# A hybrid attention and mixture-of-experts block on one core: y leaves PSUM in four blocks of 32 rows, the token sum runs in two row tiles of 64, and the expert kept outside the ring is number 23

## The reference, cut to what matters

```python
def _moe(x, router_w, router_bias, w_gate, w_up, w_down, sh_gate, sh_up, sh_down):
    ...
    def body(acc, blk):
        tok, w, e = blk
        xb = xf[tok]
        h = jax.nn.silu(xb @ w_gate[e]) * (xb @ w_up[e])
        return acc.at[tok].add((h @ w_down[e]) * w[:, None]), None
    ...
    shared = (jax.nn.silu(xf @ sh_gate) * (xf @ sh_up)) @ sh_down
    return (routed + shared).reshape(B, S, D)

for layer in range(2):
    h = mixer(x)
    x = _layer_norm(ALPHA * x + h, ...)
    f = _moe(x, ...)
    x = _layer_norm(ALPHA * x + f, ...)
```

## Time and profile before

| | us |
|---|---|
| median of three runs | 1326.66 (1326.54 to 1328.49) |
| the profiled execution, its own time | 1328.11 |
| its span in the trace | 1326.30 |
| TensorE busy | 1206.6 (91%) |
| DVE, ACT busy | 365.1 (28%), 257.3 (19%) |
| gate/up matmuls (L755), busy | 460.5 + 14.1 |
| down matmuls (L780), busy | 233.8 + 7.3 |
| DMA | 444.39 MB, 335 GB/s over the span |

### The profile page before, as it was taken

How to read it: one execution, slowest core, us unless ns; L and a number is a source line. 1 busy time by engine, 2 the same in 40 slices (tenths; PEclk the granted TensorE clock), 3 DMA queues, 4 the chain that set the end, 5 groups by cost and what they waited for, 6 DMA issues and landing times.

```text
span 1326.3 us, 15983 instructions
## 1 busy us (share of the span) xinstructions
PE 1206.6 (91%) x6187; PEld 556.8 (42%) x6187; DVE 365.1 (28%) x741; ACT 257.3 (19%) x544; POOL 16.0 (1%) x22
## 2 busy tenths in 40 slices
PE   8989999999999998999878799999999998999984
PEld 4556453433434343434344654443434344343431
DVE  0575451212112121212142436321212121111214
ACT  1343221111111111112102632121111111111110
POOL 0000000000000000000010001000000000000000
PEclk9996999999999999999979899999999999999997
DMA  9345439999999999999863406599999999999991
GB/s 338 77 171 242 166 129 380 420 419 420 420 419 420 421 420 422 420 421 420 334 248 127 190 2 261 218 420 418 420 421 419 419 420 421 420 421 420 421 379 64
DMA packets 67728, 444.39 MB, mean 335 GB/s; under 512 B 7648, under 2 KB 12128, under 8 KB 16352
## 3 DMA queue, kind: packets, MB, share of 16 engines
q1 hardware_dynamic: 67680, 443.71, 82.1%
HBM read 442.63 MB, written 1.05 MB: 335 GB/s over the span
## 4 chain that ended last, share of the span: by engine, by line
PE 86%; DVE 5%; issue 5%; ACT 4%; POOL 1%; DMA 0%; POOLq 0%; DVEq 0%; SPq 0%
PE psum L755 34%; PE psum L780 17%; PE psum L714 5%; PE psum L874 4%; PE psum L619 4%; PE psum L806 4%; PE psum L790 2%; PE psum L554 2%; DVE room L1629 2%; PE psum L642 2%; PE psum L1015 2%; ACT room L1170 1%; PE psum L1041 1%; PE psum L727 1%; PE psum L595 1%
## 5 line engine op out<-in xcount | busy, mean ns | idle before, releaser
L755 PE MATMUL psum<-ring,arena 128*64 128x512 f32 x2016 | 460.5, 602 | 35.6 <-issue 35.6
L755 PEld LDWEIGHTS psum<-ring,arena 128*64 128x64 f32 x2016 | 165.1, 139 | 321.1 <-issue 320.8
L780 PE MATMUL psum<-ring,room 128*64 128x512 f32 x1008 | 233.8, 598 | 3.6 <-issue 1.7
L1638 DVE TENSOR_TENSOR y_low<-psum,y_high 128x1024 fp32r<-128x1024 f32 x64 | 78.4, 1225 | 367.4 <-ACT y_high L1163 367.4
L1629 DVE SCALAR_TENSOR_TENSOR room<-room,arena,psum 128x256 f32<-128x256 f32 x64 | 30.7, 480 | 375.9 <-ACT room L1170 375.9
L780 PEld LDWEIGHTS psum<-ring,room 128*64 128x64 f32 x1008 | 73.4, 136 | 132.6 <-issue 118.7
L1163 ACT CAST y_high<-psum 128x1024 fp32r<-128x1024 f32 x64 | 64.8, 1012 | 253.3 <-PE psum L780 253.3
L1170 ACT ACTIVATE room<-psum 128x256 f32<-128x256 f32 x64 | 24.6, 385 | 424.3 <-PE psum L755 424.3
L806 PE MATMUL psum<-y_high,spread 32*128 32x512 f32 x512 | 64.9, 496 | 5.0 <-issue 4.9
L714 PE MATMUL psum<-onehot,x_high 128*128 128x256 f32 x256 | 65.7, 297 | 0.0
L714 PE MATMUL psum<-onehot,x_low 128*128 128x256 f32 x256 | 63.0, 283 | 0.0
(11 more groups left out here) (232 smaller groups left out, 901.9 us busy)
## 6 DMA issues: line engine op xcount, KB each, us to landing
ring<-in_expert_w_gate SPq DMA_DIRECT2D x126, 1024.0 KB, 14.4
ring<-in_expert_w_up SPq DMA_DIRECT2D x126, 1024.0 KB, 17.1
ring<-in_expert_w_down SPq DMA_DIRECT2D x126, 1024.0 KB, 17.0
ring<-in_swa_nsa_w_in SPq DMA_DIRECT2D x8, 1036.0 KB, 14.1
room<-in_swa_nsa_w_out SPq DMA_DIRECT2D x1, 4096.0 KB, 14.2
room<-in_mla_w_out SPq DMA_DIRECT2D x1, 4096.0 KB, 20.7
ring<-in_mla_w_in SPq DMA_DIRECT2D x1, 2688.0 KB, 10.9
ring<-in_mla_w_uq SPq DMA_DIRECT2D x1, 2304.0 KB, 8.8
```

The costliest lines, as they stand in the source:

```text
L755: mm = pe.matmul(BANK[2][CAP * e:CAP * e + CAP, :], xg[:, c, 2 * j + e, :], expert(stored[e])[0][:, c], start=c == 0, stop=c == KC - 1)
L780: mm = pe.matmul(PS[0][CAP * e:CAP * e + CAP, half * 512:(half + 1) * 512], ht[:, c, CAP * e:CAP * e + CAP], expert(stored[e])[1][:, c, ha ...
L1638: V.tensor_tensor(ylo, PS[0][:, :], yhi.bitcast(F32), ALU.subtract).then_inc(sem[f"yd_dve{L}"], 1)
```

## The change

1. `y_high` and `y_low` are made in four blocks of 32 rows each (`Y_ROWS`). A block comes from rows ordered by expert, then chunk, and goes to rows ordered by chunk, then expert. Two of the four blocks change place.
2. The token sum takes two row tiles of 64 rows, one per chunk, in place of four of 32. `spread` is 128 tokens wide instead of 256, and the token numbers in the table count within a chunk. In each turn one half of the width is summed.
3. The expert kept outside the ring is `KEPT` = 5*4+3 = 23, the second expert of pair 11, instead of 63. Round 5 of the refills leaves out slot 3, the last round loads both.
4. The first refill of gate and up is issued in two halves, after chunk 3 and after chunk 7 of pair 0; `gu_pe` is counted four times a pair.
5. The load semaphores are one for each pair of slots instead of one for each slot.

```diff
+KEPT_ROUND = SHARED_DOWN * 2 + 1
+KEPT = KEPT_ROUND * 4 + 3
...
+        Y_ROWS = [(slice(CAP * u + WIN * e, CAP * u + WIN * e + WIN), slice(CAP * e + WIN * u, CAP * e + WIN * u + WIN))
+                  for u in range(TC) for e in range(2)]
...
+        def expert_half(sp, L, k, e, half):
+            for i, w in enumerate((e_gate, e_up)):
+                at, n = i * KC * DE, KC // 2 * DE
+                sp.dma_start(slot[k][:, at + half * n:at + (half + 1) * n],
+                             w[L, e].rearrange("(p c) f -> p (c f)", c=KC)[:, half * n:(half + 1) * n])\
+                  .then_inc(sem[f"gu{k // 2}_in{L}"], 16)
...
             def refill(i, kept=None):
                 for j in range(NPAIR):
                     mine = [k for k in (2 * j, 2 * j + 1) if k != kept]
-                    sp.wait_ge(sem[f"gu_pe{L}"], (i * NPAIR + j + 1) * 2)
-                    for k in mine:
-                        expert_gate_up(sp, L, k, ((i + 1) * NSLOT + k) % NE)
+                    if isinstance(i, int) and i == 0 and j == 0:
+                        for half in range(2):
+                            sp.wait_ge(sem[f"gu_pe{L}"], 2 * half + 2)
+                            for k in mine:
+                                expert_half(sp, L, k, NSLOT + k, half)
+                    else:
+                        sp.wait_ge(sem[f"gu_pe{L}"], (i * NPAIR + j + 1) * 4)
+                        for k in mine:
+                            expert_gate_up(sp, L, k, ((i + 1) * NSLOT + k) % NE)
...
-            with sp.Fori(0, n_rounds - 2) as i:
+            refill(0)
+            with sp.Fori(1, KEPT_ROUND - 1) as i:
                 refill(i)
-            refill(n_rounds - 2, NSLOT - 1)
+            refill(KEPT_ROUND - 1, NSLOT - 1)
+            with sp.Fori(KEPT_ROUND, n_rounds - 1) as i:
+                refill(i)
...
-            load_gate_up(sp, keep, e_gate[L, NE - 1], e_up[L, NE - 1], sem["keep_gu_in"])
-            load_down(sp, keep, e_down[L, NE - 1], sem["keep_dn_in"])
+            load_gate_up(sp, keep, e_gate[L, KEPT], e_up[L, KEPT], sem["keep_gu_in"])
+            load_down(sp, keep, e_down[L, KEPT], sem["keep_dn_in"])
...
             for part in (yhi, ylo):
-                for q in range(4):
-                    tc, half, rows = q % TC, (q // TC + turn + j) % 2, slice(WIN * q, WIN * (q + 1))
-                    mm = pe.matmul(ACC[tc][:, half * 512:(half + 1) * 512], spread[rows, j, tc * P:(tc + 1) * P],
-                                   part[rows, half * 512:(half + 1) * 512],
...
+                for tc in range(TC):
+                    rows = slice(CAP * tc, CAP * (tc + 1))
+                    mm = pe.matmul(ACC[tc][:, turn * 512:(turn + 1) * 512], spread[rows, j, :],
+                                   part[rows, turn * 512:(turn + 1) * 512],
...
-                nc.scalar.copy(yhi, PS[0][:, :]).then_inc(sem[f"ya_act{L}"], 1)
+                for there, here in Y_ROWS:
+                    nc.scalar.copy(yhi[there, :], PS[0][here, :]).then_inc(sem[f"ya_act{L}"], 1)
...
                     for e in range(2):
                         half = slice(CAP * e, CAP * e + CAP)
-                        V.tensor_copy(gslot[half, :, 1], got[half, :, e, 2])
+                        for u in range(TC):
+                            there, here = CAP * u + WIN * e, CAP * e + WIN * u
+                            V.tensor_copy(gslot[there:there + WIN, :, 1], got[here:here + WIN, :, e, 2])
...
-                    dve.wait_ge(sem[f"ya_act{L}"], p + 1)
-                    V.tensor_tensor(ylo, PS[0][:, :], yhi.bitcast(F32), ALU.subtract).then_inc(sem[f"yd_dve{L}"], 1)
+                    for n, (there, here) in enumerate(Y_ROWS):
+                        dve.wait_ge(sem[f"ya_act{L}"], p * 4 + n + 1)
+                        ins = V.tensor_tensor(ylo[there, :], PS[0][here, :], yhi.bitcast(F32)[there, :], ALU.subtract)
+                    ins.then_inc(sem[f"yd_dve{L}"], 1)
```

More of the change, by code:

```diff
@@ L115 @@
 EACH = ["pick_dve", "slots_pe", "gates_dve", "gather_pe", "xhi_act", "xlo_dve", "xg_act", "xg_dve",
-        "gu_pe", "silu_act", "h_dve", "spread_dve", "ht_pe", "ht_act", "down_pe", "ya_act", "yd_dve", "half_pe", "comb_pe"] + [f"{part}{k}_in" for part in ("gu", "dn") for k in range(NSLOT)]
+        "gu_pe", "silu_act", "h_dve", "spread_dve", "ht_pe", "ht_act", "down_pe", "ya_act", "yd_dve", "half_pe", "comb_pe"] + [f"{part}{k}_in" for part in ("gu", "dn") for k in range(NPAIR)]
 SEMS = (
@@ L676, in groups @@
         def groups(eng, L, group):
-            group(0, False)
+            group(0, False, False)
             eng.wait_ge(sem["groups_dve"], L + 1)
@@ L730, in pe_slots, with kept, missing, pe_gate_up @@
             mm.then_inc(sem[f"slots_pe{L}"], 1)
-        def pe_gate_up(pe, L, i, j, last):
+        def kept(i, j):
+            return isinstance(i, int) and i == SHARED_DOWN and j == GP - 1
+        def missing(i, j, beyond):
+            return int((beyond and j % NPAIR == 1) or kept(i, j))
+        def pe_gate_up(pe, L, i, j, beyond):
             p, turn = i * GP + j, i * (GP // NPAIR) + j // NPAIR
             stored = [slot[j % NPAIR * 2 + e] for e in range(2)]
[L736 to L741, removed]
+            if kept(i, j):
+                stored[1] = keep
+                pe.wait_ge(sem["keep_gu_in"], BOTH["keep_gu_in"] * (L + 1))
+            halves = 64 if j % NPAIR == 0 and not (isinstance(turn, int) and turn == 0) else 0
+            pe.wait_ge(sem[f"gu{j % NPAIR}_in{L}"], (turn + 1) * 64 + halves - 32 * missing(i, j, beyond))
             first = isinstance(p, int) and p == 0
@@ L764, in pe_down @@
             stored = [slot[j % NPAIR * 2 + e] for e in range(2)]
[L765 to L770, removed]
+            if kept(i, j):
+                stored[1] = keep
+                pe.wait_ge(sem["keep_dn_in"], BOTH["keep_dn_in"] * (L + 1))
+            pe.wait_ge(sem[f"dn{j % NPAIR}_in{L}"], (turn + 1) * 32 - 16 * missing(i, j, beyond))
             if j == GP - 1 and not last:
@@ L819, in pe_experts, with group @@
             pe_shared_turns(pe, L)
-            def group(i, last):
+            def group(i, last, beyond):
                 for j in range(GP):
@@ L826, in group @@
                     before = (j - 1) % 2
-                    pe_gate_up(pe, L, i, j, last)
+                    pe_gate_up(pe, L, i, j, beyond)
                     if shared_step(i, j, SHARED_DOWN):
@@ L838, in group @@
                         pe_combine(pe, L, p - 1, before, 1)
-                    pe_down(pe, L, i, j, last)
+                    pe_down(pe, L, i, j, last, beyond)
             n_groups = groups(pe, L, group)
```

34 lines of the change are left out of this document (17 added, 17 removed).

## The result

The changed kernel takes **1331.13 us** (median of 20 runs), the kernel before beside it 1326.55 us: **0.35% slower**, ratio 1.0035 (95% interval 1.0023 to 1.0046). The predicted time was 1326.5 us, 0.2 less than before; the measured one lies inside the range, but on the side to which the prediction had given 0.34, and above the 1329.7 that its own case allowed. The profiled execution took 1333.83 us, its span is 1332.1.

What follows compares the result with a forecast made beforehand. The weights' stream was taken to bound a layer once the preloaded experts are used, TensorE at both ends. Terms -4.8 + 3.7 + 0.7 + 0.5 - 0.2 = -0.1 us a layer gave 1326.5 us, range 1320.5 to 1333.5.

Steps and rivals of the forecast that it cites:

- the two large holes: Weights' stream behind pair 11: waits of 2.1 and 2.2 us for free slots, near 358 and 375.
- The first refill: Start of a layer: issuing half the gate/up refill after chunk 3 brings the stream forward, -2.4 us a layer.
- The clock: TensorE at a layer's end: half rate at pair 31 (0.7) and the last combine (0.5), +1.2 us a layer.
- the hole of 1.1 us: Weights' stream near 213: pair 3's load waits for free slots, leaving 2.4 of the 3.5 us gained.
- Rival 4: First refill: the early half brings nothing, as smaller loads flow worse or SP is late; +2.3 a layer, 1331; 9%.
- The kept expert: Expert 23 kept instead of 63: -2.2 us a layer; stream loses 4.6 us; both stream edits start pair 31 4.8 earlier.
- Rival 3: Stream behind pair 11: its lead is kept, the 4.6 us loss shrinks to 0 to 1.6; more likely about 1321; 16%.
- The four blocks: Making y in blocks of 32 rows: hidden in the middle, +3.7 us a layer at its end only.
- Rival 2: Making y: blocks cost more than the whole, from shared PSUM bank reads or rows changing place; +8 a layer, 1343; 6%.
- The two row tiles: Combine: half as many matmuls of twice the rows run side by side, about -0.2 us a layer.
- rival 1: Combine: the two row tiles of 64 do not overlap; +3.4 a layer, 1333; 11%.
- Tiny gate copies: DVE under the gather: two copies added a group, 0.16 us each, costing nothing.

Runs made afterwards that it cites:

- experiment 4: Changed kernel with the first refill issued whole again, after chunk 7 of pair 0: 1331.12 us, ratio 1.0034 to the kernel before.
- experiment 9: Changed kernel with all eight half loads of the first refill issued late, after chunk 7 of pair 0: 1336.02 us, ratio 1.009 to the kernel before.
- experiment 6: Changed kernel with y in one piece, four row tiles of 32 and number 31 kept instead of 23: 1310.23 us, ratio 0.9883 to the kernel before.
- experiment 7: Changed kernel with y in one piece, four row tiles of 32, number 31 kept and the first refill whole: 1315.07 us, ratio 0.9919.
- experiment 8: Changed kernel with six matmuls on constants filling the wait before the last combine: 1327.2 us, ratio 1.0016 to the kernel before.
- experiment 1: Changed kernel with y, gate copies, spread and token sum as before (parts 1 and 2 undone): 1319.66 us, ratio 0.9952 to the kernel before.
- experiment 2: Kernel before with only the blocks of y and the two row tiles added (parts 1 and 2): 1332.17 us, ratio 1.0049.
- experiment 5: Changed kernel with number 31, second expert of pair 15, kept in place of number 23: 1320.83 us, ratio 0.9963 to the kernel before.

## Why the prediction was wrong

The structure was right: the gains ahead of pair 31 and the costs behind it, the two large holes, the cover in the middle. What failed is the size of two terms, the first refill and the clock, and both errors fell on one side.

- **The first refill, -2.4.** "The eight half loads take SP some 0.45 us each, against 1.25 us of transfer each: no hole." The first was issued at 196.65 (197.1 forecast) and SP took 0.33 to 0.85 us for each, which is no bound. The 1.25 us of transfer was taken from the flow of whole loads, 420 GB/s. The half loads flow at 254 to 337, so pair 10 came at 140.3 and not at 138.55 (331.7 - 193.15), and the hole of 1.1 us that the prediction had subtracted is not there. In place of 2.4 the term measured 0.3 us (experiment 4), and 0.2 to 1.7 over all traces; experiment 9 shows the slow flow as the cause, at 2.1 to 2.3 us. Rival 4 named this ("the smaller loads flow worse") at 9%, and its 1331 is the measured time. That is luck in part: it had priced only this error, of which 1.2 us reached pair 31, and the clock made up the rest. In experiments 6 and 7 the half refill did bring 1.2 and 1.7. The flow over 198 to 212 was 318 GB/s in the changed kernel, 347 in experiment 8, which runs the same instructions there, and 356 in experiment 6, with pair 10 at 140.3, 139.5 and 139.4: so it varies between executions, and why stays open.
- **The kept expert** (headed -2.2; the working gives -4.8 with the refill, so -2.4). The 4.6 us of holes are 4.1, the two large ones at the forecast places. With the first term, pair 31 was to be 4.8 us earlier and is 3.6 to 3.7: 1.8 us too late at pair 10, less 0.5 that the holes are smaller. Rival 3 falls with the holes. Of the 3.6, 1.7 is what pair 30 no longer loses to its half rate and pair 31 loses in its place.
- **The four blocks, +3.7.** +3.68. Hidden in the middle, as the rows at 383.17 to 390.99 show. Rival 2 falls: a block costs 1.21 to 1.23 us whether its rows change place or not, with ACT reading the same bank. Four take 4.92 us, so no two overlap, as was forecast.
- **The two row tiles.** They overlap (0.50 us for both); rival 1 falls. They bring nothing either: the turn is 0.74 us as before, and the 0.2 that I took for it is not in the trace. No run has the row tiles without the blocks, so this rests on the rows alone.
- **The clock, +1.2.** It was +2.6: 1.7 for pair 31 (I took 0.7) and 0.94 for the last combine (0.5). The prediction averaged over two outcomes whose price it knew, "0 or 1.7" and "0 to 0.9"; both came at their upper end, in both layers of this trace. For pair 31 that is this execution's: in experiment 8 it runs at half rate in layer 0 and at full rate in layer 1. For the combine that was no chance: after 6.10 us all 16 last combines of the eight kernels with that wait run at half rate from the first matmul, and experiment 8 removes it by filling the wait. The Trainium skill (TensorE: Matmul & The Clock Gate, Why this matters for your kernels) warns of gaps between bursts; the trace agrees (0.80 for 0.50 behind 6.10 us), and the prediction should have taken its upper bound here.
- **Tiny gate copies, "nothing".** They lengthen the gather by 0.3 us: pair 4 starts at 55.5, before at 55.2, and with the copies alone at 55.6. After pair 7 the stream hides it.

Sum for layer 0: -3.6 + 1.7 + 3.7 + 0.9 = +2.7, against +2.93 measured and -0.1 predicted; the 1.2 us of pair 31's start (the first refill, less the smaller holes), 1.4 of the clock and 0.2 of the combine make 2.8 of the 3.0 between them. The other 0.2 lies between pair 31's start and y, and no run explains it.

Two things make the change slower, and either alone, put right, makes it faster. One is the blocks, 4.6 us at the end of each layer (experiments 1 and 2). The other is that part 3 was placed where the ring could not hold what it gave, which the prediction had seen and priced. Pair 10 holds TensorE for 6.6 us more, the expert saved at pair 11 puts the stream another 7.5 us ahead, and the ring holds two pairs. Four pairs later the same saving is kept (experiment 5).

## What to carry to other kernels

Where a stream of loads bounds a stretch, a load saved is worth only what the buffers can hold at that point: work out the lead there, and put the saving away from any step in which the consumer is late (here 7.5 us saved brought 3.4 at pair 11 and about 7 four pairs later, from pair 10 to pair 30). An epilogue chopped into blocks by partitions costs its full length for each block; it hides behind the next tile and returns at the last one, together with the clock of what follows. When a DMA share reads 1.0, read the GB/s beside it.

## What the runs showed of the hardware that I had not expected

- **Flow at a share of 0.93 to 1.03**, in windows of 4 us. Loads of 1 MB over 128 partitions in pieces of 8 KB: 393 to 428 GB/s (experiment 4). 512 KB over 128 partitions in pieces of 4 KB: 235 to 340 (experiment 9). 512 KB over every second partition in pieces of 8 KB: 350 to 401. 512 KB over 64 neighbouring partitions: 203 to 211.
- **The clock after a short wait.** After some 2.4 us of idleness the last combine ran at full rate throughout in 3 of 10 layers (both of the kernel before, layer 0 of experiment 1), and fell to half at its start or within it in the other 7.
- **Pair starts and the half rate.** Which pair runs at 8.78 us moves with small shifts: pair 30 in both layers before, none of the last two in experiment 2, pair 31 in both layers of the change. Some 2 us a layer of any comparison of two traces can be this; the attention stage, untouched, took 167.72 to 172.73 us among the traces.
